# Hybrid encoder trunk on one core: the sample streams' matrix states kept compact and moved into the delta-rule loop, the head norm cut in two, w_out's first chunks placed between its steps

## What is computed

```python
x = x + 0.5 * rmsnorm(swiglu(rmsnorm(x, g[0]), ...), g[1])
u = rmsnorm(x, g[2]) @ w_in            # split among four head groups
...                                     # A: pooling  B: RWKV-7  C: short convolution  D: stick-breaking attention
x = x + rmsnorm(concat(A, B, C, D) @ w_out, g[3])
x = x + 0.5 * rmsnorm(swiglu(rmsnorm(x, g[4]), ...), g[5])
```

```python
s_kk = S @ kk_t
S = S * w_t - outer(s_kk, kk_t * a_t) + outer(v_t, k_t)
y_t = S @ r_t
```

## Time and profile before

| what | value |
|---|---|
| median of 3 runs | 2930.69 us (2930.13 to 2931.51) |
| the profiled execution | 2932.16 us, span 2930.4 us, mean granted TensorE clock 0.948 |
| PE busy | 2723.6 us (93%), 20686 matmuls |
| DVE busy | 996.9 us (34%) |
| ACT busy | 762.4 us (26%) |
| POOL busy | 915.0 us (31%) |
| DMA | 188.36 MB in 356051 packets, mean 64 GB/s |

### The profile page before, as it was taken

How to read it: one execution, slowest core, us unless ns; L and a number is a source line. 1 busy time by engine, 2 the same in 40 slices (tenths; PEclk the granted TensorE clock), 3 DMA queues, 4 the chain that set the end, 5 groups by cost and what they waited for, 6 DMA issues and landing times.

```text
span 2930.4 us, 47913 instructions
## 1 busy us (share of the span) xinstructions
PE 2723.6 (93%) x20686; PEld 2647.8 (90%) x20686; DVE 996.9 (34%) x1484; ACT 762.4 (26%) x1063; POOL 915.0 (31%) x452
## 2 busy tenths in 40 slices
PE   6999999898878899999989999989987798999997
PEld 6999999897777899999989999989967588999997
DVE  5222201765533622220152221047646345222103
ACT  3222211323311322221232222233142123222211
POOL 4333332532111433333243333343311124333331
PEclk8999999998779899999999999999979799999998
DMA  3222222223001122222212222222220011222221
GB/s 96 72 72 73 75 73 74 66 66 96 2 10 44 51 72 78 72 70 78 75 51 72 78 72 74 73 62 71 65 77 3 16 58 51 79 72 72 74 74 62
DMA packets 356051, 188.36 MB, mean 64 GB/s; under 512 B 16330, under 2 KB 354086, under 8 KB 355912
## 3 DMA queue, kind: packets, MB, share of 16 engines
q1 hardware_dynamic: 355668, 186.25, 21.9%
q10 hardware_dynamic: 244, 0.08, 0.0%
HBM read 179.50 MB, written 6.80 MB: 64 GB/s over the span
## 4 chain that ended last, share of the span: by engine, by line
PE 86%; DVE 7%; issue 2%; DVEq 2%; ACT 1%; POOL 1%; ACTq 1%; DMA 0%; POOLq 0%; SPq 0%
PE ps L1430 26%; PE ps L1432 25%; PE ps L1431 25%; PE ps L1424 2%; DVE h_split L964 1%; DVE xT L957 1%; PE ps L1837 1%; PE ps L1833 1%; PE ps L1823 1%; DVEq L956 1%; PE ps L1587 1%; PE ps L1449 1%; POOL w_lo L518 0%; PE ps L1581 0%; PE ps L1919 0%
## 5 line engine op out<-in xcount | busy, mean ns | idle before, releaser
L518 POOL TENSOR_TENSOR w_lo<-w_raw,w_hi 128x1024 fp32r<-128x1024 f32 (+1 forms) x330 | 786.6, 2385 | 1594.6 <-ACT w_hi L590 1591.6
L1430 PE MATMUL ps<-h_split,w_hi 128*128 128x384 f32 (+1 forms) x3808 | 1211.3, 318 | 67.1 <-POOL w_lo L518 44.8
L1432 PE MATMUL ps<-h_split,w_lo 128*128 128x384 f32 (+1 forms) x3808 | 1194.4, 314 | 0.0
L1431 PE MATMUL ps<-h_split,w_hi 128*128 128x384 f32 (+1 forms) x3808 | 1185.9, 311 | 0.0
L1430 PEld LDWEIGHTS ps<-h_split,w_hi 128*128 128x128 f32 x3808 | 727.0, 191 | 79.9 <-POOL w_lo L518 41.8
L1432 PEld LDWEIGHTS ps<-h_split,w_lo 128*128 128x128 f32 x3808 | 732.8, 192 | 0.0
L1431 PEld LDWEIGHTS ps<-h_split,w_hi 128*128 128x128 f32 x3808 | 728.4, 191 | 1.3
L590 ACT ACTIVATE w_hi<-w_raw 128x1024 fp32r<-128x1024 f32 (+1 forms) x330 | 342.1, 1037 | 870.3 <-DMA w_raw<-in_ffn_w_down 395.8
L1430 PE MATMUL ps<-hidden_split,w_hi 128*128 128x384 f32 (+1 forms) x1344 | 419.8, 312 | 0.0
L1432 PE MATMUL ps<-hidden_split,w_lo 128*128 128x384 f32 (+1 forms) x1344 | 416.7, 310 | 0.0
L1431 PE MATMUL ps<-hidden_split,w_hi 128*128 128x384 f32 (+1 forms) x1344 | 413.3, 308 | 0.0
(11 more groups left out here) (299 smaller groups left out, 1833.4 us busy)
## 6 DMA issues: line engine op xcount, KB each, us to landing
w_raw<-in_ffn_w_gate SPq DMA_DIRECT2D x88, 512.0 KB, 3.8
w_raw<-in_ffn_w_up SPq DMA_DIRECT2D x88, 512.0 KB, 3.8
w_raw<-in_ffn_w_down SPq DMA_DIRECT2D x64, 448.0 KB, 3.7
w_raw<-in_w_in SPq DMA_DIRECT2D x42, 512.0 KB, 4.0
w_raw<-in_ffn_w_down SPq DMA_DIRECT2D x32, 512.0 KB, 3.9
w_raw<-in_w_out SPq DMA_DIRECT2D x16, 512.0 KB, 4.0
token_rows<-in_x_prompt SPq DMA_DIRECT2D x4, 512.0 KB, 5.6
k_cache<-in_cache_sb_k SPq DMA_DIRECT2D x2, 1024.0 KB, 7.4
```

The source lines that it names most:

```text
L518: nc.gpsimd.tensor_tensor(WLO[s][:, 0:n], RAW[s][:, 0:n], WHI[s][:, 0:n].bitcast(F32), ALU.subtract).then_inc(sem(f"lo_ready{s}"), 1)
L1430: MM(out, hi, mov[:, 0, cols], start=first, stop=False)
L1431: MM(out, hi, mov[:, 1, cols], start=False, stop=False)
L1432: return MM(out, lo, mov[:, 0, cols], start=False, stop=last)
```

## The change

It does these things, and the computation stays the same:

- The samples' states are compact: `SNC` and `STC` hold 8 x 2 x 64 columns with the two heads of a pair on the two halves of the partitions, and no zeros. `SNC` lies over the rows of v in `XS`, `STC` over `BA`. POOL's zeroing goes. SP loads them after `values_turned`.
- In the samples' tile's slots, PE turns the states (k = 1), multiplies them with alpha and rho in one matmul (k = 3), and adds the value products (k = 5). ACT copies the turned states (k = 2) and the right-hand side (k = 4). DVE folds gate, `ln_w` and `ln_b` into the bonus and the gate (k = 1 and 3) and decays the states (k = 4).
- Spreads of u and the values are one instruction each over four streams a half; the state update is 16 matmuls with 256 columns.
- The head norm is done for the prompt's 512 tokens and for the samples' 128 apart, each with its own step names.
- w_out's blocks 0 and 1, without chunks 2 and 3, are done three chunks at a time between these steps.
- The turns of the new states, sample and prompt, come after chunks 2 and 3 of both blocks, into PSUM banks 5 to 7; SP's stores of them come after the load of w_out's fifth block, and DVE waits for the stores ahead of its fifth y tile in place of its first.

The core of the diff:

```diff
@@ tiles
-        SN = SBF[:, 0:NSTR * G].rearrange("p (b g n) -> p b g n", b=NSTR, g=GC)
+        SNC = XSF[:, 4 * T:4 * T + NSTR * GC * HD].rearrange("p (b g n) -> p b g n", b=NSTR, g=GC)
+        STC = BA[:].rearrange("p g t -> p (g t)")[:, 0:NSTR * GC * HD].rearrange("p (b g n) -> p b g n", b=NSTR, g=GC)
@@ SP
-                sp.wait_ge(sem("sn_zeroed"), l + 1)
+                sp.wait_ge(sem("values_turned"), nth(l, "values_turned"))
...
-                sp.wait_ge(sem("prompt_state_out"), nth(l, "prompt_state_out"))
-                sp.dma_start(io["p_wkv"][l, 0].rearrange("h v k -> v h k"), TOK[0:CH, 2, 0, :].rearrange("v (h k) -> v h k", h=NH)).then_inc(sem("wkv_stored"), 16)
+                load_block(out_block(l) + 4, w_out_v[l, :, :, 4 * P:5 * P])
                 sp.wait_ge(sem("sample_state_out"), nth(l, "sample_state_out"))
...
+                sp.wait_ge(sem("prompt_state_out"), nth(l, "prompt_state_out"))
...
-                for m in range(4, DC):
+                for m in range(5, DC):
@@ POOL
-                pool.wait_ge(sem("mv_out"), (l + 1) * TT)
-                nc.gpsimd.memset(SN.rearrange("p b g n -> p (b g n)"), 0.0)
...
+                pool.wait_ge(sem("values_out"), nth(l, "values_out"))
                 pool.wait_ge(sem("exps_ready"), (l + 1) * len(PAIRS))
...
+                nc.gpsimd.tensor_tensor(NMK, value_rows(PT).rearrange("p (h n) -> p h n", h=NH).unsqueeze(2).broadcast_to([P, NH, HSTR, HD]),
+                                        ROWM.unsqueeze(1).unsqueeze(3).broadcast_to([P, NH, HSTR, HD]), ALU.mult).then_inc(sem("kappa_spread"), 1)
@@ ACT, intra
+                    if p == 2 and update and v == 0:
+                        act.wait_ge(sem("stateT_in"), nth(l, "stateT_in"))
+                        A(STC.rearrange("p b g n -> p (b g n)"), PSF[:, 6 * 512:8 * 512], ACT.Copy).then_inc(sem("stateT_out"), 1)
+                    if p == 2 and update and v == 1:
+                        act.wait_ge(sem("state_rhs_in"), nth(l, "state_rhs_in"))
...
@@ DVE, y_tiles
+                    if e % 3 == 1 and m == 4:
+                        dve.wait_ge(sem("wkv_stored"), (e // 3 + 1) * 5 * 16)
@@ DVE, intra
+                        if p == 2 and v < GC:
+                            V.scalar_tensor_tensor(out=BV[:, v, :], in0=BV[:, v, :], scalar=vec(l, "ln_b", v), in1=GA[:, v, :], op0=ALU.add, op1=ALU.mult)
+                            V.tensor_scalar(GA[:, v, :], GA[:, v, :], vec(l, "ln_w", v), None, ALU.mult)
                         return
...
+                    if p == 2 and v == 1:
+                        dve.wait_ge(sem("state_rhs_in"), nth(l, "state_rhs_in"))
+                        V.tensor_tensor(STC, STC, PCX[:].rearrange("p g b -> p b g").unsqueeze(3).broadcast_to([P, NSTR, GC, HD]), ALU.mult)
@@ DVE, tail (all of it new; centre, invert and normed are the former instructions on a part of the tokens)
+                dve.wait_ge(sem("mean_in"), nth(l, "mean_in"))
+                centre(PARTS[0], MEANS[0]).then_inc(sem("centred"), 1)
                 dve.wait_ge(sem("u_done"), (l + 1) * (CHUNKS + 1))
...
+                V.tensor_tensor(CSP[:, :, PARTS[0]], CSP[:, :, PARTS[0]], GA[:, :, PARTS[0]], ALU.mult)
+                dve.wait_ge(sem("sample_mean_in"), nth(l, "sample_mean_in"))
+                centre(PARTS[1], MEANS[1]).then_inc(sem("sample_centred"), 1)
...
+                dve.wait_ge(sem("sample_delta"), l + 1)
...
                 fence().then_inc(sem("sample_states"), 1)
...
                 dve.wait_ge(sem("inverse_spread"), nth(l, "inverse_spread"))
...
+                normed(PARTS[0], SPREADS[0]).then_inc(sem("yr_ready"), 1)
+                dve.wait_ge(sem("sample_inverse_spread"), nth(l, "sample_inverse_spread"))
+                normed(PARTS[1], SPREADS[1]).then_inc(sem("sample_yr_ready"), 1)
@@ PE, new functions called from intra in the slots k = 1, 3, 5 of the samples' tile
+                def states_turned():
...
+                    pe.wait_ge(sem("wkv_loaded"), (l + 1) * 4 * 16)
+                    for b in range(NSTR):
+                        for g in range(GC):
+                            for e in range(2):
+                                at = 6 * 512 + (b * GC + g) * HD
+                                end = MM(PSF[half(e), at:at + HD], SNC[half(e), b, g, :], IDENT[half(e), half(e)], start=True, stop=True)
...
+                def state_products():
...
+                                out = PS[half(e), 6 + c, 0:2 * P].rearrange("p (w g n) -> p w g n", w=2, g=GC)[:, :, g, at:at + TS]
+                                end = MM(out, STC[half(e), b, g, :], AR[half(e), g, :, b * TS:(b + 1) * TS], start=g == 0 and b % HSTR == 0, stop=False, skip_group_check=True)
...
+                def kappa_values():
...
+                        if p == 2:
+                            (states_turned, state_products, kappa_values)[v]()
@@ PE, tail
+                pe.wait_ge(sem("yr_out"), l * (CHUNKS + 1) + CHUNKS)
+                pe.wait_ge(sem("mv_out"), (l + 1) * TT)
+                for g in range(GC):
+                    end = MM(PS[:, 4 + g, :], HEADS, CSP[:, g, 0:TP], start=True, stop=True)
...
+                out_chunks(0, others[:3])
...
+                for w, spread_rows in enumerate((NMU, NMK)):
+                    for h, g, e, hc, pr in heads():
+                        for c in (0, 1):
+                            end = MM(PS[pr, 2 + c, g * G:(g + 1) * G], TOK[half(c), 0, w, hc], spread_rows[half(c), h].rearrange("p s n -> p (s n)"),
+                                     start=w == 0 and g == 0, stop=w == 1, skip_group_check=True)
...
+                out_chunks(0, others[3:])
...
+                pe.wait_ge(sem("sample_states"), nth(l, "sample_states"))
+                block_ready(b0 + 1)
+                out_chunks(1, others[:3])
...
+                out_chunks(1, others[3:])
...
                 pe.wait_ge(sem("mixed"), nth(l, "mixed"))
```

More of the change, by code:

```diff
@@ new lines, in invert, with normed @@
+                def invert(cols):
+                    V.reciprocal(HCOLS[:, cols], HCOLS[:, cols])
+                    fence()
+                    n = cols.stop - cols.start
+                    V.tensor_copy(INV_ROWS[:, cols.start * HD:cols.stop * HD].rearrange("p (i n) -> p i n", n=HD), HCOLS[:, cols].unsqueeze(2).broadcast_to([P, n, HD]))
+                    return fence()
+                def normed(ts, spread):
+                    V.tensor_tensor(SCR[:, :, ts], spread, CSP[:, :, ts], ALU.mult)
+                    fence()
+                    V.tensor_tensor(SCR[:, :, ts], SCR[:, :, ts], BV[:, :, ts], ALU.add)
+                    return fence()
@@ L1396, in _ @@
+                invert(slice(PT * NH, TT * NH)).then_inc(sem("sample_inverse_rows"), 1)
                 dve.wait_ge(sem("inverse_spread"), nth(l, "inverse_spread"))
[L1397 to L1401 removed]
@@ L1923, in _ @@
                 end.then_inc(sem("rhs_in"), 1)
+                pe.wait_ge(sem("yr_out"), l * (CHUNKS + 1) + CHUNKS)
+                pe.wait_ge(sem("mv_out"), (l + 1) * TT)
+                for g in range(GC):
+                    end = MM(PS[:, 4 + g, :], HEADS, CSP[:, g, 0:TP], start=True, stop=True)
+                end.then_inc(sem("mean_in"), 1)
+                pe.wait_ge(sem("state_ready"), (l + 1) * CHUNKS)
                 pe.wait_ge(sem("rhs_ready"), (l + 1) * (CHUNKS + 1))
@@ new lines, in _ @@
+                end.then_inc(sem("sample_delta"), 1)
+                out_chunks(0, others[3:])
+                pe.wait_ge(sem("sample_centred"), nth(l, "sample_centred"))
+                for g in range(GC):
+                    at = G + g * 2
+                    end = MM(PS[:, 6, at:at + 2], SCR[:, g, TP:T], HEADS[:, 0:P:HD], start=True, stop=True)
+                end.then_inc(sem("sample_var_in"), 1)
+                pe.wait_ge(sem("sample_states"), nth(l, "sample_states"))
+                block_ready(b0 + 1)
@@ new lines, in _ @@
+                out_chunks(1, others[:3])
+                pe.wait_ge(sem("inverse_rows"), nth(l, "inverse_rows"))
+                for g in range(GC):
+                    for i in range(PT):
+                        end = turn(PS[:, 4 + g, i * P:(i + 1) * P], INV_ROWS[:, i * G + g * P:i * G + (g + 1) * P])
+                end.then_inc(sem("inverse_spread"), 1)
+                pe.wait_ge(sem("sample_inverse_rows"), nth(l, "sample_inverse_rows"))
+                for g in range(GC):
+                    end = turn(PS[:, 7, g * P:(g + 1) * P], INV_ROWS[:, PT * G + g * P:PT * G + (g + 1) * P])
@@ L1977, in _ @@
                     used(end, b0 + m)
+                for b in range(NSTR):
+                    for g in range(GC):
+                        for e in range(2):
+                            at = 6 * 512 + (b * GC + g) * HD
+                            end = MM(PSF[half(e), at:at + HD], STC[half(e), b, g, :], IDENT[half(e), half(e)], start=True, stop=True)
+                end.then_inc(sem("sample_state_in"), 1)
+                for g in range(GC):
```

(2 more changed lines are left out.)

210 lines of the change are left out of this document (76 added, 134 removed).

## The result

The changed kernel takes **2846.45 us** (median of 4 runs, 2841.48 to 2848.32) against 2930.41 us of the kernel before beside it (median of 4): a ratio of 0.971, 95% interval 0.969 to 0.973. The forecast was 2842.5 us, with a range of 2833 to 2867.

What follows compares the result with a forecast made beforehand. It saw PE, busy 93%, bound in the tail by a relay of late runners with no engine full. Removing 142.5 us and adding 54.3 gains 88.2, so 2842.5 us against the median, range 2833 to 2867.

Steps and rivals of the forecast that it cites:

- the choice of the level: PE's clock in the tail: taken as 2.4 GHz throughout; at 1.2 GHz it would cost 11 us more a layer.
- Rival 1: Clock stays low in the tail between the chain's last product and w_out's chunks 2 and 3: 2864.5 us, chance 0.18.
- Rival 3: States still land as late as before, so PE stands in the loop: 21.4 us a layer, 2885 us, chance 0.01.
- Price of a plain f32 matmul: PE's loop and tail: sixteen 64x64 matmuls priced at 0.5 us (2.4 GHz) or 0.85 (1.2 GHz), variance products at 0.11 each.
- State update: Tail on PE: 16 matmuls of 256 columns, 2.1 us running two at a time, 4.3 one after another.
- rival 2: State update does not run in pairs and the loop pays its upper bound: 2849.7 us, chance 0.22.
- Tail: From the chain's last product to PE's start on w_out's chunks 2 and 3: 21.8 us a layer, against 71.37 and 71.15.
- Slots: Sample tile's slots at the loop's end grow by 4.4 us in layer 0 and 3.7 in layer 1; bounds 1.2 and 5.5.
- POOL's spread at 0: POOL's single spread beside DVE's chain steps in the loop: could add 0.9 us a layer, counted as 0.
- The last wait: PE's 2.6 us wait at the tail's end for DVE's last leg, ahead of w_out's chunks 2 and 3.
- After "mixed": Behind the operand for w_out's chunks 2 and 3: turns back add 1.3 us a layer; later loads and stores add nothing.
- rival 4: Slower: the last wait drops the clock through w_out's other six blocks, 47.8 us a layer, 2938 us, chance 0.01.

Runs made afterwards that it cites:

- chunks last: Changed kernel with w_out's 12 interleaved chunk products all put behind the last inverse turns, right ahead of the wait for mixed: 2856.03 us.
- one norm: Changed kernel with the head norm in one part again over 640 columns, its means behind the sample's own outputs: 2855.34 us.
- decay later: Changed kernel with DVE's decay of the compact states behind the chain's RHS sum in place of ahead of it: 2846.67 us, beside 2847.43 for the changed kernel.
- Inverse first: Changed kernel with the prompt's eight inverse turns ahead of the third group of three w_out products in place of behind it: 2838.49 us.
- turned early: Changed kernel with the 32 state turns ahead of PE's wait for the masked scores: 2852.73 us, beside 2847.43 for the changed kernel.
- four moves: Changed kernel with inverse turns ahead of the third group, decay behind the RHS sum, state turns ahead of the scores' wait, and POOL's value spread late: 2832.04 us.
- the changed kernel's second profile: The changed kernel run again without edits, as reference for later runs: 2847.43 us, slots 24.11 and 27.87 us in layers 0 and 1.
- states after loop: Changed kernel with state turns, state products, kappa products, ACT's two copies and the decay moved out of the sample slots, between loop and tail: 2847.59 us.

## Why the prediction was right, and where its terms were off

**Direction, mechanism and the choice of the level held.** Before, the tail was a relay of late runners at a mean clock of 0.74; after, it is at 1.00 in both layers. Rival 1 (a low clock) did not come, though "chunks last" and "one norm" show that it was near. Rival 3 (late states) did not come either: the loads were issued at 757.03, only just ahead of the loop (its first scores start at 760.23), but 74 us ahead of the turns that need them (831.12).

**The sum** was 88.2 us of gain; the stretches give 82.2 (41.4 and 40.8), so its terms were 6.0 too good. The other 3.2 of the measured 85.4 came from outside the stretches. I put that down to the spread between executions: what lies behind layer 0's block 2, without layer 1's stretch, took 1905.1 to 1911.7 us in the twelve profiles from the changed kernel on, with the same code there. That these 3.2 us made up for half of the error of the terms is luck.

- *Price of a plain f32 matmul: the step that failed.* I counted "32 turns of 64x64" as two runs of 16 records at 0.85, and eight variances at 0.11. In the trace such a matmul leaves **two** records: L2011 is issued 32 times and shows x64, L1943 twice and shows x4; a turn by L1429 leaves one (ten, x10). (The x32 of L1914 before, which I also took for 32 products, are sixteen.) So means took 1.92 us (forecast 1.0), variances 1.70 (0.9), sample means 0.62 (0.25), state turns 3.0 (1.7), state products 1.85 (1.0), and the turns back with the prompt's 2.17 (1.3). The last is 0.9 a layer beside the tail.
- *State update:* 1.89 us (860.04 to 861.93) against 2.1, so rival 2 fell. The reason I gave was off. L1943 shows 0.96 us for one f32 matmul of 512 columns, so 0.48 for 256 and 7.7 for the sixteen in series; 1.89 is a fourth of it, which fits four quadrants at once rather than two; that offset the doubled count.
- *Tail:* 23.1 us a layer against 21.8. DVE's last leg began 1.7 us late, for the reason above; it took 5.3 (868.9 to 874.2), forecast 5.7, up to PE's start.
- *Slots:* 4.67 us longer in layer 0 (forecast 4.4), 5.07 in layer 1 (3.7). In layer 0 the pieces (3.0, 1.85, 0.5 and the decay's 1.2) add up to 6.6, of which 4.7 shows. The low level was shorter in return: by the windows' means 3.7 us of the slots were at 0.50 (0.93 over 26.20), against 6.9 before (0.84 over 21.50), worth 1.6 of the 1.9. In layer 1 I had taken the high level; its turns took as long as layer 0's:

```profile
2230.76 3.07 PE L1819 MATMUL ps<-consts,xs 64*64 64x64 f32 x64
...
2238.89 1.86 PE L1831 MATMUL ps<-alpha_rho,kk_a 64*64 64x32 f32 x58
...
2244.55 0.59 PE L1909 MATMUL ps<-rhs,invT 64*64 64x64 f32 x7 [1.92 <-DVE rhs L1351]
```

- *Decay on the path:* right, shown by "decay later" at 1.1 to 1.4 us a layer.
- *POOL's spread at 0:* right here, by luck. I argued that the chain step beside it reads PSUM. The step that does was not slowed, but behind it comes one on SBUF alone, which I had left out; in the changed kernel the late turns kept DVE idle while POOL ran (832.75 to 834.64). Once they moved, that step met POOL and cost 1.2 us, and the clock after it more.
- *The last wait:* forecast 2.6 us, measured 2.50, and I took it as DVE's. "Inverse first" shows that it was PE's order: DVE had the operand at 864.5, PE turned it at 867.81.
- *After "mixed":* 5.25 us of rule rows against 5.23 before, counted as unchanged, rightly. No fall of w_out's later blocks (rival 4).
- *The drain between tiling modes,* the rule of the Trainium skill (TensorEngine Tiling (Array Packing), section Key Properties) that I had set against the trace: L1435's 128x128 product starts at 854.96, before L1955's 64x64 ones end at 855.03 (854.55 + 0.48, an end that the profile models), and in the same way at all five changes of the tail. The product after that one starts 0.28 us later, as against 0.27 behind L1986, where the tile does not change. Here page and measurement differ: no cost of a drain is seen.

## What to carry to other kernels

Take work that needs no late operand out of a relay, in its compact form; whether it then stands in an earlier loop or just ahead of the relay may be worth nothing, so measure the parts apart. Where PE waits, compare the time at which the operand was ready with the place at which PE's own order asks for it: one move of eight turns was worth 8 us. Price matmuls by records per issued instruction, and ask of every filled gap which two engines it newly sets side by side.

## What was unexpected of the hardware

The granted clock decided more than some of the work moved. In the sample tile's slots it fell in different places: behind PE's wait of 2.97 us (changed kernel), behind one of 1.93 ("turned early", low for 16 us although PE was busy all of 838 to 844), behind one of 1.91, or not at all ("four moves"). In one layer of the changed kernel's second profile it fell behind both the 2.97 and a 1.92. The same wait of 2.5 us ahead of "mixed" was followed by a fall in both profiles of the changed kernel, by none in "states after loop", and by one in a single layer of "decay later". Why some of these waits brought it down and others did not is left open.

A VectorE instruction on SBUF of 0.29 us took 1.50 beside a GpSimd one of 1.88 us; one that also reads PSUM was not slowed beside it. And a plain f32 matmul leaves two records in the trace where a turn by L1429 leaves one.
